# Constant products between the gate and up strips of the last expert group, and slot numbers taken ahead of the wait for up weights

## What is computed

```python
def hier_moe(h, w_rg, b_rg, w_re, b_re, w_gate, w_up, w_down):      # first block, D_EXPERT = 128
    ...
    for e in range(N_EXPERTS):                                       # 32 experts
        hid = jax.nn.silu(xf @ w_gate[e]) * (xf @ w_up[e])
        y = y + combine[:, e:e + 1] * (hid @ w_down[e]).astype(f32)

def reference(x, ...):
    x = first_block(x, ...)       # GLA + sparse attention, then hier_moe
    return second_block(x, ...)   # forgetting + dilated attention, then hierarchical_moe, D_EXPERT_2 = 512
```

## Time and profile before

| | us |
|---|---|
| median of 3 runs | 923.46 |
| the three runs | 921.35, 923.46, 927.38 |
| profiled execution | 919.98 |
| its span (first to last record) | 918.2 |
| granted TensorE clock, mean | 0.952 |

### The profile page before, as it was taken

How to read it: one execution, slowest core, us unless ns; L and a number is a source line. 1 busy time by engine, 2 the same in 40 slices (tenths; PEclk the granted TensorE clock), 3 DMA queues, 4 the chain that set the end, 5 groups by cost and what they waited for, 6 DMA issues and landing times.

```text
span 918.2 us, 22060 instructions
## 1 busy us (share of the span) xinstructions
PE 768.1 (84%) x9739; PEld 595.4 (65%) x9739; DVE 301.7 (33%) x752; ACT 207.8 (23%) x441; POOL 68.9 (8%) x76
## 2 busy tenths in 40 slices
PE   7999999999999899999998878767675576756764
PEld 4888888777777568867657667546464454645543
DVE  2676722453543365875333111101010010010101
ACT  2113332321422244436533101001020010100100
POOL 6200020000100030450000000000000000000000
PEclk9999999999999999999999999988898998897988
DMA  9996556356899998462678999999999999999995
GB/s 303 327 348 225 210 176 240 135 215 244 318 407 406 401 352 327 147 263 93 250 283 337 427 423 427 425 428 426 431 425 431 428 429 428 429 428 429 428 428 236
DMA packets 55561, 310.22 MB, mean 338 GB/s; under 512 B 5426, under 2 KB 7178, under 8 KB 43088
## 3 DMA queue, kind: packets, MB, share of 16 engines
q1 hardware_dynamic: 50704, 301.07, 82.2%
q0 software_dynamic: 2912, 4.37, 1.6%
q10 hardware_dynamic: 1888, 3.94, 1.1%
HBM read 307.77 MB, written 4.19 MB: 340 GB/s over the span
## 4 chain that ended last, share of the span: by engine, by line
PE 58%; DMA 33%; DVE 3%; issue 3%; ACT 1%; DVEq 0%; SPq 0%; ACTq 0%
PE ps L2080 55%; DMA ring<-in_w_up 25%; DMA ring<-in_w_down 5%; DMA ring<-in_w_gate 3%; PE ps L2106 1%; PE ps L2253 1%; PE ps L2441 0%; DMA xx<-in_x 0%; ACT y_high_words L1011 0%; DVE arena L1627 0%; PE ps L2120 0%; DVE ring L1569 0%; PE ps L2213 0%; PE ps L2488 0%; DVE arena L1416 0%
## 5 line engine op out<-in xcount | busy, mean ns | idle before, releaser
L2080 PE MATMUL ps<-ring,arena 128*32 128x128 f32 (+3 forms) x4944 | 245.7, 318 | 91.1 <-DMA ring<-in_w_gate 43.5
L2080 PEld LDWEIGHTS ps<-ring,arena 128*32 128x32 f32 (+1 forms) x4944 | 191.2, 126 | 140.6 <-DMA ring<-in_w_gate 51.9
L2080 PE MATMUL ps<-arena 32*128 32x256 f32 (+9 forms) x1476 | 129.4, 345 | 3.1 <-issue 2.4
L2080 PEld LDWEIGHTS ps<-arena 32*128 32x128 f32 (+5 forms) x1476 | 97.4, 162 | 29.8 <-issue 21.6
L2080 PE MATMUL ps<-ring,const 128*32 128x256 f32 x864 | 57.5, 408 | 28.9 <-DMA ring<-in_w_down 25.5
L2080 PE MATMUL ps<-ring,xx 128*128 128x256 f32 (+2 forms) x312 | 80.0, 409 | 0.8 <-issue 0.6
L2080 PE MATMUL ps<-xx,ring 128*128 128x256 f32 x352 | 78.8, 381 | 0.0
L2080 PEld LDWEIGHTS ps<-xx,ring 128*128 128x128 f32 x352 | 65.9, 190 | 9.6 <-issue 0.7
L2080 PEld LDWEIGHTS ps<-ring,xx 128*128 128x128 f32 x312 | 58.4, 190 | 15.9 <-issue 6.5
L2080 PEld LDWEIGHTS ps<-ring,const 128*32 128x32 f32 x864 | 27.9, 115 | 54.4 <-issue 37.7
L1639 DVE TENSOR_TENSOR w_fa<-g_dil,ps 128x128 f32<-128x128 f32 x16 | 4.6, 288 | 136.8 <-ACT g_dil L999 136.8
(11 more groups left out here) (348 smaller groups left out, 807.6 us busy)
## 6 DMA issues: line engine op xcount, KB each, us to landing
ring<-in_w_gate SPq DMA_DIRECT2D x36, 2048.0 KB, 23.6
ring<-in_w_up SPq DMA_DIRECT2D x36, 2048.0 KB, 25.1
ring<-in_w_down SPq DMA_DIRECT2D x33, 2048.0 KB, 23.9
ring<-in_w_in SPq DMA_DIRECT2D x15, 2048.0 KB, 21.9
arena<-in_w_down SPq DMA_DIRECT2D x5, 2048.0 KB, 7.9
ring<-in_w_out SPq DMA_DIRECT2D x4, 2048.0 KB, 8.4
arena<-in_w_gate SPq DMA_DIRECT2D x4, 2048.0 KB, 12.7
arena<-in_w_up SPq DMA_DIRECT2D x3, 2048.0 KB, 11.5
```

The costliest lines, as they stand in the source:

```text
L2080: ins = pe.matmul(dst, w, x, start=start, stop=stop, skip_group_check=True)
```

## The change

Two edits in PE's program. `slot_tokens` moves ahead of `arrived` for the up chunk, in every group. A new helper `keep_busy(n)` issues n products of the identity with a constant matrix (both 128x128) into the first 128 columns of bank 7, which the up strips overwrite. It is called with 14 between `slot_tokens` and `arrived`, in the loop body's second half only, that is for group 7.

```diff
+                def keep_busy(n):
+
+                    for _ in range(n):
+                        mm(bank(7, P), ident, before, True, True)
+
                 def group(n, c, q, half, nth=0):
...
                     for i in range(2):
+                        if i == 1:
+                            slot_tokens(n, half)
+                        if i == 1 and not isinstance(n, int) and half == 1:
+                            keep_busy(14)
                         arrived(c[i], q, nth)
                         w4 = slot4(c[i])
-                        if i == 1:
-                            slot_tokens(n, half)
                         ins = strips(6 + i, lambda k, j: xg[:, k, j * SLOTS:(j + 1) * SLOTS],
```

## The result

| | before | changed |
|---|---|---|
| median, us | 920.75 (20 runs) | 927.12 (20 runs) |
| lowest | 919.07 | 919.13 |
| profiled execution | 919.98 | 929.17 |
| its span | 918.2 | 927.4 |

The ratio of changed to before is 1.0053, 95% interval 1.0033 to 1.0072. It is not the quotient of the two medians, which are 6.37 us or 0.7% apart, since it leaves out slow runs, here three of the changed kernel (933.3, 934.05 and 4218.2 us). The kernel became slower by a half to seven tenths of a per cent. I had forecast 921.7 us, a gain of 1.8 us, with bounds of 918.7 and 925.7; the median lies above them. The lowest runs are alike, but the changed kernel's lie much wider: 919 to 934 us. Nothing in the profile speaks of the one execution of 4218.2 us, and it is left out of what follows. The median of before had been 923.46 over the first three runs and is 920.75 over 20.

What follows compares the result with a forecast made beforehand. Weight transfers by DMA were taken to bound the kernel after 490 us, PE's order in block 2 before. 3.26 us won less 1.21 and 0.25 gave 1.8, so 923.46 became 921.7 us, range 918.7 to 925.7.

Steps and rivals of the forecast that it cites:

- the sum: From group 7 to the end: 3.26 us won, less 1.21 waiting for chunk 31, less 0.25 for shape_const2, leaves 1.8.
- the entrance to block 2: At about 333 us: a microsecond won here is one at the end; one won earlier counts only if it reaches here.
- my rivals: Full gain to block 2, 920.2 us (0.13); only slot products won, 922.5 to 923.0 (0.22); slower, 924.7 (0.08).
- the 0.07 for something not in the profile: Chance of 0.07 kept for an outcome with no mechanism seen in the profile; no size given.
- The rival on the slow side: Group 7: up chunk lands before the 14 products end, so strips queue behind them; 924.7 us, at most 926.4; chance 0.08.
- the products: Ahead of group 7's up strips: 14 at 0.12 us, 1.68 in all, ending at 317.64, covered by the wait.
- where the stall goes: After group 7's up strips, three things are late next: the down chunk, DVE's weight sum of chunk 31, the shape_const2 load.
- The down chunk: Group 7: lands at 323.7 us, PE asks for it at 324.03; just there, with 0.3 us to spare.
- DVE's wait for chunk 31: Before DVE copies x for block 2: chunk lands at 329.1 us after 23.3, leaving 2.05 of the 3.26 us.
- the 0.25 us for shape_const2: POOL's 512 KB load, issued earlier, shares queues with chunk 31's last 5 us and costs 0.25 us, bounds 0 to 0.5.
- the clock in group 7: At the up strips: products keep full clock; strips take 1.89 us instead of 3.58, scatter's second half 4.24 after their start.
- the way to the end: From block 2 on: its norm at about 331.4 us, the full DMA stretch about 1.8 us earlier and as long.

Runs made afterwards that it cites:

- moved-only kernel: Slot products moved ahead of the wait for the up chunk, without the constant products, against the kernel before: 919.93 against 920.3 us (0.9974 to 1.0031).
- the copies first: DVE copies x before the weight sum of chunk 31, in three kernels against before: 919.47 against 921.43 us, 919.87 and 917.99 against 921.4.
- the late execution: Profiled execution with slot products moved, no constant products and DVE copying x before its weight sum; up chunk landed late, strips at 325.20; median 919.47 against 921.43 us.

## Why the prediction was wrong

**Step that failed: the sum had no term for what the added instructions do to the code behind them.** It put their effect after 490 us at nothing, and measured were three idle times of 6.16, 6.09 and 5.96 us there and 8.0 us more from the first gather to the end. The prediction says that after 490 us nothing that PE does *faster* moves the end, and takes from it that only the entrance to block 2 counts. It never asked what makes PE *slower* there. Here added instructions had two costs: their own time at their place, and turns of a later loop that load instructions again. The second was some 8 of the 9.2 us between the two spans, and it is enough for the whole loss of the medians: the same number of instructions without array work, or in another part of the program, gave 926.62 and 928.83. None of my rivals named it; it falls in the 0.07 for something not in the profile. The rival on the slow side (products behind the landing) is real, but worth 1 us, and its top of 926.4 lies near the measured 927.12 by luck.

**Mis-sized: the products.** 14 by 0.12 us was 1.68 us; it is 3.37. The row counts matmuls, and a float32 product is two of them: the strips of 32 products stand as x64 in the earlier trace rows, which I had before me. They ended at 320.2 rather than 317.64. 1.7 us of that is the wrong size, and the rest is that in this execution the products also began 1.0 us later than forecast (316.95 for 315.96). So they ended 1.0 us behind the landing of 319.2, and with the forecast's own start they would still have ended 0.65 us behind its landing (315.96 + 3.37 = 319.33 for 318.68).

**Right in kind, off in size: where the stall goes.** The down chunk wasn't late. DVE's wait for chunk 31 is what I had said, and decides. But I carried the 23.3 us over where 25.2 was measured, and the chunk was issued 0.6 us later as well. That size isn't there in each execution. The changed kernel with 72 or with 200 instructions more has the same first MoE; in those profiles chunk 31 took 23.3 and 23.4 us and the norm started at 331.71 and 331.74, against 331.4 forecast and 333.18 before, and the first gather came 0.7 to 0.8 us earlier than before. No run shows the 0.25 us for shape_const2 either: in these two it was issued 1.4 and 1.6 us earlier (325.25 and 325.04 for 326.63), and chunk 31 took as long as before within 0.1 us. And I hadn't seen that the idle time of PE ahead of the norm would grow from 1.20 us to 3.56 (2.01 and 2.24 in those two) and let the clock fall there. On that the rule of the Trainium skill (TensorE: Matmul & The Clock Gate, on why this matters for your kernels), no gaps over about 3 us, should have been put to the next gap too. The trace agrees with it there: 3.56 us idle, then 0.50. But in this case shorter idle times were followed by a fall too: 2.24 us with 200 instructions more (0.50 at 333 us, the norm takes 2.97 us), and 1.91 us in the moved-only kernel, behind its four slot products (0.50 at 322 us, the strips take 3.40 us).

**Right: the clock in group 7.** The strips ran in 1.9 us, and the stretch from their start to the second half of the scatter in 3.99 us (4.24 forecast). **Right: the move.** Alone it neither costs nor gains anything that these runs tell. **Right, in part: the way to the end.** With the copies first, the norm starts 2.6 to 3.4 us before the old one, and so does the gather of the second MoE (the late execution left aside). Of that the end shows 2 to 3 us by the ratios (0.9969, 0.9977, 0.9972), and 1.5 to 3.4 us by the medians (919.47, 919.87, 917.99 against 921.4).

## What to carry to other kernels

Work put into an idle time isn't free because the engine idles: it has instructions, and in a program with a long loop they can cost more at the other end of the program than at their place. Look at the instruction queue's packets inside the loops, before and after, and test a suspicion with cheap real instructions elsewhere, since register moves that nobody reads may not survive the compiler. And when a stall is cured, follow the next two waits with their landing times and leave them a margin: the same transfer, chunk 31, took 23.2 to 25.9 us in these profiles. Here three kernels with two steps on DVE reordered were 0.2 to 0.3% under before, and no product beside them has been shown to add to that.

## What the runs showed of the hardware that I had not expected

Behind the first turn, a turn of the loop of the second MoE either loads nothing or 9 packets of 16 KB. With the packets it then starts about 6 us late beside full DMA queues (what it takes beside empty ones isn't seen). Its first gather instructions take longer too, 23 of them 5.17 us against 3.84 us for 32 before, at a granted clock of 0.53 in that stretch. The switch between the two was 56 instructions ahead of the loop in an otherwise equal program; with 28, one turn of one profile loaded again.

Products of one column, 28 matmuls in 0.84 us with 1.83 us of idle time behind them, didn't keep the clock up: it was 0.50 from 321 us, and the strips took 3.24 us. Six matmuls with 256 columns in 1.54 us and 0.77 us of idle time did: it stayed at 1.00, and the strips took 1.96 us. The two differ in the idle time as well as in the products, so these runs don't say which of them counts.
